# Attention stage of a decoder trunk: softmax weights added up before one sum by ones, half of the cache pages on TensorE's column strips, pages alone on SyncE's queue

## The chip, the cores and the metric

The kernel runs on 1 core of a Trainium2 chip. The metric is the device time of one execution in microseconds. Engines by their names in the profile: PE is TensorE (PEld its weight loads), DVE VectorE, ACT ScalarE, POOL GpSimd, SP SyncE.

## What is computed

One inference step of a two-layer decoder for a prompt of 2048 rows and for 8 sample sequences of one row each. Layer 0 has attention with forgetting (8 heads of 64) beside a gated MLP; layer 1 is an mLSTM. The change lies in the attention of layer 0, in which the prompt attends to itself and each sample row to 64 pages of 128 cached positions:

```python
def fox_block(q, k, v, cq, ck, qpos, kpos):
    s = jnp.einsum('bqhd,bkhd->bhqk', q, k).astype(F32) * (q.shape[-1] ** -0.5)
    s = s + cq.swapaxes(1, 2)[:, :, :, None] - ck.swapaxes(1, 2)[:, :, None, :]
    s = jnp.where(kpos[None, :] <= qpos[:, None], s, -jnp.inf)
    p = jax.nn.softmax(s, axis=-1)
    return jnp.einsum('bhqk,bkhd->bqhd', p.astype(v.dtype), v)
# prompt: blocks of queries against the prompt's own k, v
# sample: v_all = concatenate([cache_v[page_table], v]) : 8 sequences x 64 pages x 128 positions x 512
y = jnp.concatenate([ya, yb], -1) @ w_out      # ya = att * silu(za); then the residual is added
```

## The kernel before

`build` runs `even_project` (input projection of layer 0, and the scores of the sample rows against the cached keys), `decode_softmax` (softmax of these scores, left in `keep["scores"]`: for each page and head one weight per cached position, positions on the 128 partitions), `attend`, and `mlstm` (layer 1). Only `attend` is changed. It does three things in one block, on all engines at once:

- *Prompt attention.* Queries go in 4 groups of 512 rows, heads in 4 pairs: 16 units (`UN`). A unit of group g has 4(g+1) key slots (`count`), 160 slots in all (`STEPS`). In slot i TensorE computes the scores of 128 keys by up to 512 queries for both heads of the pair into `S2` (`score_keys`, two heads on the two row halves of the array), ScalarE turns them into weights `PT` (`exp`, L992), and a slot later TensorE multiplies by the values into `O` (L1215) and sums the weights over the keys by a matrix of ones into `Z` (L1217) (`product`). Before a unit's keys come, its queries' maxima are needed: `score_queries` computes scores the other way round into `S1` (one buffer), VectorE takes maxima (`maximum`, L1050), both for the next unit, spread over the slots of this one (`p1_end`). At a unit's end `gate` multiplies `O` by the gate, `invert` makes 1/Z on ScalarE by Ln and Exp, `normalise` multiplies.
- *Output projection* of the group before (`project`, L1235, `y_at`: 24 of them in slots, 8 in a tail of 8 steps), with the `residual` added on VectorE and read and written by GpSimd's DMAs.
- *Cached values of the sample rows.* 512 pages of [128 x 512] are loaded in pairs into a ring of five (`vpage`, `RING`), multiplied by the weights and added up in `acc` by VectorE (`page_pair`, L1100 and L1103). Of every fourth pair ScalarE does the products (`scale_page`, L1007, 16 activations a pair). At a sequence's end a turn `d` sums over the partitions by ones.

Every engine's order is written out by the Python loops at build time. "Turns" are uses of TensorE's and ScalarE's shared bank `T` (transposes of staged k, q and x rows, and small sums); turn e waits for the evacuation of turn e-1. Where pages stand is set by `spare` and `pair_end`: the pairs are shared out over the slots in proportion to an estimate of TensorE's time, so that a slot with a projection has 4 pairs, others mostly 1. SyncE's queue holds in one order the loads of stage rows (ring of 4), of the values `V` and of the pages, each behind the wait for its buffer. Slots of units 4, 5, 8, 9, 12 and 13 hold the projections.

## Time and profile before

| | us |
|---|---|
| median of 3 runs | 3806.46 (3800.5 to 3808.48) |
| the profiled execution | 3808.97 |
| its span | 3806.8 |
| PE busy in the span | 3324.9 (87%) |
| DVE busy | 2084.7 (55%) |
| ACT busy | 1047.5 (28%) |

The span is from the first to the last instruction of one execution; the execution's own time is 2.2 us longer. The stage of `attend` goes from about 1058 us (first memset of GpSimd) to about 2098 us, its 160 slots from 1090 to 2018 us. The page's busy tenths show all stages in 40 slices of 95 us; `attend` lies in slices 12 to 22, and the chain that ended last lies wholly in the last stage, since the stages are parted by barriers. "Idle before" of a group is the time for which the engine stood ahead of its instructions, with who released it.

### The profile page before, as it was taken

How to read it: one execution, taken by the hardware profiler on the slowest of the kernel's cores; microseconds unless marked ns; L12 is line 12 of the kernel's file. 1: busy time of each engine (PE TensorE's matmuls, PEld its weight loads, DVE VectorE, ACT ScalarE, POOL GpSimd, SP SyncE). 2: the span in 40 equal slices, each digit the busy share in tenths (PEclk: the TensorE clock that was granted, in tenths of full speed). 3: DMA queues.
4: the chain of work that ended last, by engine and by line, in shares of the span. 5: the costliest groups of instructions: out<-in, count | busy, mean ns of one | idle time of the engine just before them, and what ended most of it. 6: DMA issues, size and time to landing. Idle time of an engine off the chain costs nothing. (4 is left out here: it accounts for less than half of the span.)

```text
span 3806.8 us, 44892 instructions
## 1 busy us (share of the span) xinstructions
PE 3324.9 (87%) x14087; PEld 1795.8 (47%) x14087; DVE 2084.7 (55%) x3066; ACT 1047.5 (28%) x2520; POOL 120.7 (3%) x221
## 2 busy tenths in 40 slices
PE   2999999999269888999888499999999999667799
PEld 1444444444134333333333276767767767412343
DVE  1778887888447776887786043443444434313211
ACT  1111111110145554554463122223222322103111
POOL 0000000000010000000000000000000000000000
PEclk8999999999679999999999699999999999877899
DMA  5566666665155644645555500000000000425232
GB/s 212 173 194 195 193 201 197 195 203 178 67 158 182 195 134 152 184 143 178 160 164 169 195 12 11 22 11 11 22 11 11 22 11 12 22 77 155 95 110 73
DMA packets 243054, 448.06 MB, mean 118 GB/s; under 512 B 38529, under 2 KB 69249, under 8 KB 241850
## 3 DMA queue, kind: packets, MB, share of 16 engines
q1 hardware_dynamic: 222602, 412.12, 35.9%
q0 software_dynamic: 5696, 18.88, 1.4%
q10 hardware_dynamic: 14592, 15.24, 1.2%
q8 instruction: 58, 0.95, 0.1%
q14 instruction: 106, 0.87, 0.1%
HBM read 390.16 MB, written 55.99 MB: 117 GB/s over the span
## 5 line engine op out<-in xcount | busy, mean ns | idle before, releaser
L523 PE MATMUL ep_PJ<-ep_w,ep_xT 128*128 128x512 f32 x1792 | 781.9, 595 | 10.4 <-ACT ep_xT L383 10.4
L523 PEld LDWEIGHTS ep_PJ<-ep_w,ep_xT 128*128 128x128 f32 x1792 | 337.5, 190 | 420.3 <-issue 413.9
L1734 PE MATMUL mb_B<-ml_w,mp_xT 128*128 128x512 f32 x1024 | 446.4, 594 | 0.0
L444 DVE TENSOR_TENSOR ep_kpage<-ep_kpage,ep_q_bc 128x1024 f32<-128x1024 f32 x256 | 311.5, 1217 | 128.9 <-DMA ep_kpage<-in_cache_k_dram 128.6
L1007 ACT ACTIVATE at_vpage<-at_vpage,g_scores 128x64 f32<-128x64 f32 x1008 | 253.1, 338 | 262.3 <-DMA at_vpage<-in_cache_v_dram 262.3
L452 DVE TENSOR_REDUCE g_scores<-ep_kpage 128x1024 f32 (+1 forms) x256 | 311.6, 1217 | 11.5 <-DVE ep_kpage L444 3.3
L1103 DVE TENSOR_TENSOR at_acc<-at_acc,at_vpage 128x1024 f32<-128x1024 f32 x240 | 293.7, 1224 | 18.3 <-ACT at_vpage L1007 8.8
L1734 PEld LDWEIGHTS mb_B<-ml_w,mp_xT 128*128 128x128 f32 x1024 | 192.0, 190 | 230.1 <-issue 229.6
L1050 DVE TENSOR_REDUCE at_mpart<-at_S 128x2 f32<-128x1024 f32 (+3 forms) x160 | 170.3, 1065 | 220.2 <-PE at_S L1172 132.1
L1747 PE MATMUL mb_B<-mp_xT,ml_w 128*128 128x128 f32 x2048 | 252.3, 289 | 0.0
L1747 PEld LDWEIGHTS mb_B<-mp_xT,ml_w 128*128 128x128 f32 x2048 | 249.8, 205 | 0.0
L2252 PE MATMUL fi_O<-ml_w,fi_yT 128*128 128x512 f32 (+1 forms) x544 | 237.6, 595 | 0.0
L1100 DVE TENSOR_TENSOR at_vpage<-at_vpage,g_scores 128x1024 f32<-128x1024 f32 x185 | 225.3, 1218 | 0.0
L992 ACT ACTIVATE at_PT<-at_S,g_negc 128x512 f32<-128x512 f32 (+3 forms) x320 | 180.6, 615 | 161.6 <-PE at_S L1200 161.2
L1190 PE MATMUL at_S<-at_QT,at_KT 64*128 64x512 f32 (+3 forms) x640 | 165.9, 596 | 58.4 <-ACT at_PT L992 58.4
L1169 PE MATMUL at_S<-at_KT,at_QT 64*128 64x512 f32 (+3 forms) x640 | 159.9, 578 | 23.8 <-DVE at_mpart L1050 23.7
L1617 DVE SCALAR_TENSOR_TENSOR mp_cv<-mp_xcT,ml_cw,mp_cv 128x128 f32<-128x128 f32 x384 | 105.1, 347 | 132.5 <-ACT mp_cv L1532 131.3
L2252 PEld LDWEIGHTS fi_O<-ml_w,fi_yT 128*128 128x128 f32 (+1 forms) x544 | 99.4, 185 | 126.6 <-issue 126.5
L1215 PE MATMUL at_O<-at_PT,at_V 128*64 128x512 f32 (+3 forms) x640 | 152.2, 554 | 2.5 <-issue 2.5
L1217 PE MATMUL at_Z<-at_PT,g_ones 128*64 128x512 f32 (+3 forms) x640 | 144.0, 528 | 0.0
L1190 PEld LDWEIGHTS at_S<-at_QT,at_KT 64*128 64x128 f32 x640 | 50.7, 190 | 160.1 <-ACT at_PT L992 94.3
L2223 DVE TENSOR_TENSOR fi_o<-fi_h,fi_O 128x512 f32<-128x512 f32 (+1 forms) x34 | 21.8, 683 | 184.3 <-PE fi_O L2252 184.3
(447 smaller groups left out, 3613.6 us busy)
## 6 DMA issues: line engine op xcount, KB each, us to landing
ep_kpage<-in_cache_k_dram SPq DMA_DIRECT2D x512, 256.0 KB, 3.0
at_vpage<-in_cache_v_dram SPq DMA_DIRECT2D x512, 256.0 KB, 3.0
ep_w<-in_even_w_in_dram SPq DMA_DIRECT2D x8, 1796.0 KB, 30.7
ml_w<-in_odd_w_in_dram SPq DMA_DIRECT2D x24, 512.0 KB
ep_x<-in_x_prompt_dram SPq DMA_DIRECT2D x16, 512.0 KB
scratch_mix<-ep_mixed SPq DMA_DIRECT2D x16, 512.0 KB, 3.0
at_stage<-scratch_mix SPq DMA_DIRECT2D x32, 256.0 KB, 3.5
at_xh<-in_x_prompt_dram POOLq DMA_DIRECT2D x32, 256.0 KB, 3.5
```

The source lines that it names most:

```text
L444: nc.vector.tensor_tensor(kpage[i][:], kpage[i][:], q_bc[r][:].unsqueeze(1).to_broadcast([P, 2, AW]), ALU.mult).then_inc(pr[i], 1)
L452: op = nc.vector.tensor_reduce(dst, kpage[i][:].rearrange("p j (h d) -> p j h d", h=AH), AX.X, ALU.add)
L523: op = nc.tensor.matmul(BANK[name][:], xT[r][:, k, :], w[:, k, COL[name]:COL[name] + 512], start=k == 0, stop=k == KC - 1)
L992: nc.scalar.activation(PT[i % 3][:, hh, 0:n], S2[:, hh, 0:n], ACT.Exp, bias=keep["negc"][:, j, h:h + 1]).then_inc(exped, 1)
L1007: op = nc.scalar.activation(part, part, ACT.Copy, scale=keep["scores"][:, k // 32, h, p:p + 1])
L1050: nc.vector.tensor_reduce(mpart[:, qi, :, b], S1[:, :, 0:width], AX.X, ALU.max).then_inc(maxed, 1)
L1100: nc.vector.tensor_tensor(split(here), split(here), w, ALU.mult).then_inc(weighed, 1)
L1103: nc.vector.tensor_tensor(here if k % 32 == 31 else acc[:], acc[:], here, ALU.add).then_inc(added, 1)
L1190: nc.tensor.matmul(S2[:, hh, 0:n], KT[rows, hp, j * P:(j + 1) * P], QT[u % 3][rows, lo:512], start=True, stop=False, skip_group_check=True)
L1734: op = nc.tensor.matmul(B[banks[m]][:], xT[:, k, :], w[:, k, col + 512 * m:col + 512 * m + 512], start=k == 0, stop=k == KC - 1)
L1747: op = nc.tensor.matmul(B[c // 4][:, (c % 4) * P:(c % 4 + 1) * P], w[:, k, c * P:(c + 1) * P], xT[:, k, :], start=k == 0, stop=k == KC - 1)
L2252: op = nc.tensor.matmul(O[2 * r + m][0:n, :], yT[r][:, k, 0:n], w[:, k, 512 * m:512 * m + 512], start=k == 0, stop=k == KC - 1)
```

## The change

The ring of `PT` goes from 3 to 2, of stage rows from 4 to 3. `psum` (in SBUF) holds the sum of a unit's weights over its slots: VectorE copies the first and adds the others (`add_up`), and a new turn `z` at the start of the next unit sums `psum` by ones once into `T`; ScalarE takes Ln and Exp from there. `L1217` goes. Of the pages two of every four stay with VectorE (128 pairs, ring of 2 pairs), all their products now on VectorE; `scale_page` goes. The other two pages, in groups of four (64 groups, ring of 3 pairs in `spage`), are multiplied on TensorE: the weights [128 x 8 heads] are the stationary operand, the page moves, and each of the four pages of a group has its own 32 columns of the array and rows of the bank `D`. At a sequence's end `pick_heads` keeps each head's own 64 columns, and the turn `d` adds them in. SyncE's queue holds pages alone; the loads of stage rows and of `V` move to GpSimd's queue, behind its masks and among the residual's reads and writes. VectorE's order within a slot changes: `add_up` of the slot before, then pages, then `gate` and further maxima.

```diff
-        RING = 5
-        PT = [s.sb(f"PT{i}", [P, 2, 512]) for i in range(3)]
-        stage = [s.sb(f"stage{i}", [P, AW]) for i in range(4)]
+        PT = [s.sb(f"PT{i}", [P, 2, 512]) for i in range(2)]
+        psum = s.sb("psum", [P, 2, 512])
+        stage = [s.sb(f"stage{i}", [P, AW]) for i in range(3)]
-        vpage = [s.sb(f"vpage{i}", [P, 2, AW]) for i in range(RING)]
+        vpage = [s.sb(f"vpage{i}", [P, 2, AW]) for i in range(2)]
+        spage = [s.sb(f"spage{i}", [P, 2, AW]) for i in range(3)]
-            n = slot2(i)[3]
             p1 = p1_end[i] - (p1_end[i - 1] if i else first[1])
-            return (n * 2.1 + n * 3.4) / 1000 + 0.3 + 1.2 * p1 + 7.1 * len(y_at[i])
+            return slot2(i)[3] * 3.9 / 1000 + 0.3 + 1.2 * p1 + 7.1 * len(y_at[i])
+        PAIRS = NB * PAGES // 4
+        GROUPS = PAIRS // 2
+        SEQ_P, SEQ_G = PAIRS // NB, GROUPS // NB
+        whole = sum(pe_us(i) for i in range(STEPS + TAIL - 3))
+            while nd < min(PAIRS, round(PAIRS * so_far / whole)) and nd <= SEQ_P * (ready + 1):
+                nd += 1
+            while ns < min(GROUPS, int(GROUPS * so_far / whole)) and ns < SEQ_G * (ready + 1):
+                ns += 1
+            loads_at[i] += [("v", d + 2) for d in in_step(d_end, i) if d + 2 < PAIRS]
+            loads_at[i] += [("s", 2 * g + r) for g in in_step(s_end, i) for r in (3, 4) if 2 * g + r < 2 * GROUPS]
+            if i == STEPS or i and i < STEPS and i == first[unit_of[i]]:
+                late[i] = [len(turns)]
+                turns.append(("z", (unit_of[i] if i < STEPS else UN) - 1, 0))
...
         def _(sp):
+            def weighed_pair(d):
+                if d >= 2:
+                    sp.wait_ge(added, d - 1)
+                    if (d - 2) % SEQ_P == SEQ_P - 1:
+                        sp.wait_ge(turned, d_turn[(d - 2) // SEQ_P] + 1)
                 for j in range(2):
+                    page(4 * d + j, vpage[d % 2][:, j, :], vp_in[d % 2])
+            def strip_pair(n):
+                if n >= 3:
+                    sp.wait_ge(paged, 4 * ((n - 3) // 2 + 1))
+                for j in range(2):
+                    page(4 * n + 2 + j, spage[n % 3][:, j, :], sp_in[n % 3])
             for i in range(STEPS + TAIL):
+                for kind, n in loads_at[i]:
+                    if kind == "v":
+                        weighed_pair(n)
+                    else:
+                        strip_pair(n)
...
         def _(pool):
+            nc.gpsimd.memset(own_head[:], 0.0).then_inc(const, 1)
+            for strip in range(4):
+                rows = slice(32 * strip, 32 * strip + 32)
+                nc.gpsimd.affine_select(out=own_head[rows, :], in_=own_head[rows, :], compare_op=ALU.not_equal, fill=1.0,
+                                        base=0, pattern=[[-1, AH]], channel_multiplier=1).then_inc(const, 1)
+            for i in range(STEPS + TAIL):
+                while got < len(loads) and loads[got] < t_end[min(i + 2, STEPS + TAIL)]:
+                    stage_in(got)
+                    got += 1
+                if i % 8 == 0 and 1 <= i // 8 < GR:
+                    values_in(i // 8)
+                for y in y_at[i]:
+                    residual_out(y)
+                    if y + 2 < 2 * NT:
+                        residual_in(y + 2)
...
         def _(act):
+                elif kind == "z":
+                    if a:
+                        act.wait_ge(gated, a)
+                    nc.scalar.activation(rc[:], T[:], ACT.Ln).then_inc(evac, 1)
+                    act.wait_ge(evac, e + 1)
+                    nc.scalar.activation(rc[:], rc[:], ACT.Exp, scale=-1.0).then_inc(inverted, 1)
             def exp(i):
-                if i >= 3:
-                    act.wait_ge(used, 2 * (i - 2))
+                if i >= 2:
+                    act.wait_ge(used, 2 * (i - 1))
+                    act.wait_ge(summed, i - 1)
             for i in range(STEPS):
-                if i > 1 and i - 1 == first[unit_of[i - 1]]:
-                    invert(unit_of[i - 1] - 1)
                 exp(i)
+                for e in held:
+                    evacuate(e)
+                held = late[i] if turns[t_end[i + 1] - 1][0] == "z" else []
-                for k, j in scale_at[i]:
-                    scale_page(k, j)
...
         def _(dve):
+            def add_up(i):
+                u, j, lo, n = slot2(i)
+                dve.wait_ge(exped, 2 * (i + 1))
+                if j == 0:
+                    if u:
+                        dve.wait_ge(turned, z_turn[u - 1] + 1)
+                    nc.vector.tensor_copy(psum[:], PT[i % 2][:]).then_inc(summed, 1)
+                else:
+                    dve.wait_ge(summed, i)
+                    nc.vector.tensor_tensor(psum[:, :, lo:512], psum[:, :, lo:512], PT[i % 2][:, :, 0:n], ALU.add).then_inc(summed, 1)
+            def pick_heads(b):
+                dve.wait_ge(paged, 4 * SEQ_G * (b + 1))
+                nc.vector.tensor_tensor(strip_sum[:].rearrange("p (h d) -> p h d", h=AH), D[:].rearrange("p (h d) -> p h d", h=AH),
+                                        own_head[:].unsqueeze(2).to_broadcast([P, AH, AD]), ALU.mult).then_inc(masked, 1)
+                for n in todo[:1]:
+                    maximum(n)
+                if 1 <= i <= STEPS:
+                    add_up(i - 1)
+                if 1 < i < STEPS and i - 1 == first[unit_of[i - 1]]:
+                    normalise(unit_of[i - 1] - 1)
+                for d in in_step(d_end, i):
+                    page_pair(d)
+                for b in range(NB):
+                    if closed[b] == i:
+                        pick_heads(b)
+                if i == STEPS or i and i < STEPS and i == first[unit_of[i]]:
+                    gate((unit_of[i] if i < STEPS else UN) - 1)
+                if i == STEPS:
                     normalise(UN - 1)
+                for n in todo[1:]:
+                    maximum(n)
...
         def _(pe):
+                elif kind == "z":
+                    pe.wait_ge(summed, first[a + 1])
+                    for hh, rows in enumerate(halves):
+                        op = nc.tensor.matmul(T[rows, :], keep["ones"][:, 0:AD], psum[:, hh, :], start=True, stop=True, skip_group_check=True)
-                for hh, rows in enumerate(halves):
-                    nc.tensor.matmul(Z[rows, lo:512], keep["ones"][:, 0:AD], PT[i % 3][:, hh, 0:n], start=j == 0, stop=last,
                                      skip_group_check=True).then_inc(used, 1)
+            def strips(g):
+                b = g // SEQ_G
+                if g % SEQ_G == 0:
+                    pe.wait_ge(masked, b + 1)
+                for r in range(2):
+                    n = 2 * g + r
+                    pe.wait_ge(sp_in[n % 3], 32 * (n // 3 + 1))
+                for strip in range(4):
+                    n, j = 2 * g + strip // 2, strip % 2
+                    p = (4 * n + 2 + j) % PAGES
+                    op = nc.tensor.matmul(D[32 * strip:32 * strip + AH, :], keep["scores"][:, b, :, p], spage[n % 3][:, j, :],
+                                          start=g % SEQ_G == 0, stop=g % SEQ_G == SEQ_G - 1, skip_group_check=True)
+                    op.then_inc(paged, 1)
                 for y in y_at[i]:
                     project(y)
+                for g in in_step(s_end, i):
+                    strips(g)
                 if i:
                     product(i - 1)
```

## Rows read from the trace of the kernel before

**Rows 1.** Busy time of the engines in stretches, clock, DMA share, GB/s.
```profile
core 0: us, PE busy (x) PEld busy (x) DVE busy (x) ACT busy (x) POOL busy (x), PEclk, DMA share, GB/s
1380.00:1574.00 194.00, 166.55 (x734) 67.56 (x736) 132.71 (x132) 86.19 (x260) 8.72 (x16) 0.93 0.53 160
sum 1040.00, PE 915.51 PEld 382.06 DVE 745.46 ACT 527.04 POOL 44.49; mean PE 83.23 PEld 34.73 DVE 67.77 ACT 47.91 POOL 4.04
```
**Rows 2.** Groups by line, 1055 to 2095 us: busy us, mean ns | idle before.
```profile
L1103 DVE TENSOR_TENSOR at_acc<-at_acc,at_vpage 128x1024 f32<-128x1024 f32 x240 | 293.7, 1224 | 18.3 <-ACT at_vpage L1007 8.8
L1007 ACT ACTIVATE at_vpage<-at_vpage,g_scores 128x64 f32<-128x64 f32 x1008 | 253.1, 338 | 262.3 <-DMA at_vpage<-in_cache_v_dram 262.3
L1100 DVE TENSOR_TENSOR at_vpage<-at_vpage,g_scores 128x1024 f32<-128x1024 f32 x185 | 225.3, 1218 | 0.0
L1050 DVE TENSOR_REDUCE at_mpart<-at_S 128x2 f32<-128x1024 f32 (+3 forms) x160 | 170.3, 1065 | 220.2 <-PE at_S L1172 132.1 <-PE at_S L1179 87.3
L1217 PE MATMUL at_Z<-at_PT,g_ones 128*64 128x512 f32 (+3 forms) x640 | 144.0, 528 | 0.0
```
**Rows 3.** TensorE's waits, 1090 to 2020 us: us in total, times, longest.
```profile
PE at_S L1190 <- ACT at_PT L992: 58.4, 28, 6.6
PE at_S L1169 <- DVE at_mpart L1050: 21.3, 33, 2.6
```
**Rows 4.** Timeline of a late page in slot 50: start, us, instruction.
```profile
1397.33 2.02 ACT L1007 ACTIVATE at_vpage<-at_vpage,g_scores 128x64 f32<-128x64 f32 x8 [5.60 <-DMA at_vpage<-in_cache_v_dram]
1400.55 2.08 PE L1190 MATMUL at_S<-at_QT,at_KT 64*128 64x512 f32 x4 [5.79 <-ACT at_PT L992]
```
**Rows 5.** Timeline of a warm plain slot, 1588 to 1593 us.
```profile
1588.13 1.13 PE L1190 MATMUL at_S<-at_QT,at_KT 64*128 64x512 f32 x4
1589.54 1.27 ACT L992 ACTIVATE at_PT<-at_S,g_negc 128x512 f32<-128x512 f32 x2 [2.57 <-PE at_S L1200]
1590.48 1.08 PE L1215 MATMUL at_O<-at_PT,at_V 128*64 128x512 f32 x4
1591.39 1.03 PE L1217 MATMUL at_Z<-at_PT,g_ones 128*64 128x512 f32 x4
1592.35 1.13 PE L1190 MATMUL at_S<-at_QT,at_KT 64*128 64x512 f32 x4
```
**Rows 6.** Timeline of the sample rows' projection on four column strips.
```profile
59.68 1.07 PE L288 MATMUL ep_PJ<-ep_w,ep_xT 128*8 128x512 f32 x8
60.55 0.59 PE L288 MATMUL ep_TR<-ep_w,ep_xT 128*8 128x512 f32 x1
```
**Rows 7.** Timeline: a table load in an inversion, and the first tail projection.
```profile
1580.20 1.28 ACT L1000 ACT_TABLE_LOAD   x1
2030.81 5.27 PE L1235 MATMUL at_Y<-g_w_out,at_yA 128*128 128x512 f32 x8 [10.64 <-DVE at_yA L1084]
```
**Rows 8.** Timeline of the stage's start.
```profile
1058.63 2.65 SPq L889 DMA_DIRECT2D at_stage<-out_k_prompt_dram  x4
1062.00 1.11 PE L1156 MATMUL at_T<-g_ident,at_stage 128*128 128x128 f32 x4 [20.67 <-DMA at_stage<-out_k_prompt_dram]
1066.06 2.15 POOL L943 TENSOR_SCALAR_AFFINE_SELECT at_sel<-at_sel 64x128 bf16<-64x128 bf16 x8
1068.16 1.18 POOL L949 DMA_DIRECT2D at_xh<-in_x_prompt_dram  x2
```
**Rows 9.** Timeline from a projection's last matmuls to the next residual's read.
```profile
1409.05 3.60 PE L1235 MATMUL at_Y<-g_w_out,at_yB 128*128 128x512 f32 x8
...
1414.94 0.68 DVE L1108 TENSOR_TENSOR at_xh<-at_xh,at_Y 128x512 f32<-128x512 f32 x1
...
1415.91 0.54 POOL L955 DMA_DIRECT2D scratch_h<-at_xh  x1 [110.26 <-DVE at_xh L1108]
...
1419.50 0.55 POOL L949 DMA_DIRECT2D at_xh<-in_x_prompt_dram  x1 [3.04 <-DMA scratch_h<-at_xh]
```
**Rows 10.** SyncE issuing eight pages; a stage load's size and time to landing.
```profile
1199.20 8.05 SPq L901 DMA_DIRECT2D at_vpage<-in_cache_v_dram  x8
...
at_stage<-out_k_prompt_dram SPq DMA_DIRECT2D x16, 256.0 KB, 3.6
```

More of the change, by code:

```diff
@@ L903, in _ @@
[L903 to L916 removed]
+            sp.wait_ge(pages_in, 16)
@@ L1002, in scale_page @@
[L1002 to L1008 removed]
+                    nc.scalar.activation(PT[i % 2][:, hh, 0:n], S2[:, hh, 0:n], ACT.Exp, bias=keep["negc"][:, j, h:h + 1]).then_inc(exped, 1)
@@ L1247, in _ @@
                     score_queries(n)
-                here = list(range(t_end[i], t_end[i + 1]))
-                for e in here:
-                    if turns[e][0] != "m":
+                for e in range(t_end[i], t_end[i + 1]):
+                    if e not in late[i]:
                         turn(e)
@@ L1257, in _ @@
                     score_queries(n)
-                for e in here:
-                    if turns[e][0] == "m":
-                        turn(e)
+                for e in late[i]:
+                    turn(e)
             product(STEPS - 1)
```

226 lines of the change are left out of this document (95 added, 131 removed).

## Prediction

> **What bounds the kernel now.** I read the span first (3806.8 us, one core), then the busy tenths of the page: only the stage of `attend`, from 1058 to 2098 us, has the lines of the change. Over these 1040 us TensorE is busy 915.5, VectorE 745.5, ScalarE 527.0 us, at a granted clock of 0.93 in the stretch from 1380 to 1574 [rows 1]. So TensorE sets the pace, but not alone: some 125 us of the stage it stands, and part of the time it runs at 1.2 GHz. Next the groups, for the prices of one instruction [rows 2]. Then the waits inside the 160 key slots (1090 to 2020): TensorE waited 58.4 us for ScalarE's exponentials and 21.3 us for VectorE's maxima [rows 3]. The exponentials are not slow; what stands ahead of them on ScalarE is. In the timeline `scale_page` gets its page 5.60 us late, the exponential behind it is late, TensorE's `score_keys` starts after 5.79 us of idling, and its four matmuls then take 2.08 us [rows 4] where a warm slot's take 1.13 [rows 5]: each such wait also costs clock. Going through the 28 waits in the timeline, all but about 2 us follow a scaled page.
>
> A warm plain slot of full width takes 4.22 us from `score_keys` to `score_keys`: 1588.13 to 1592.35, of it `L1217`, the sum by ones, from its middle at 1591.39 to the next slot, 0.96 us with the change of weights [rows 5]. Slots with an output projection take 7.0 us more.
>
> **The change, part by part.**
>
> *Sum by ones off TensorE's slots.* Widths of all 160 slots add up to 136 full ones; 136 x 0.96 = 131 us, 128 with the shorter gaps of the narrow slots: -128 us. Back comes one sum for a unit, 16 x 0.96 = +15 us.
>
> *Strips.* 64 groups of four matmuls, [128 x 8] weights, 512 float32 columns, in column strips 0, 32, 64, 96. The trace has such a group: in the sample rows' projection four matmuls (eight instructions) start at 59.68 and the next strip group at 60.55: 0.87 us for four, not for one [rows 6]. With 0.1 us for the change of tile form (a slot's sum by ones takes 0.96, 0.09 over 0.87) a group costs 0.97: 60 of them lie in the slots, +58 us. Closing a sequence takes 12 instead of 8 one-column matmuls, each with a full weight load: about 0.9 us more, 8 times, +7 us. TensorE's work in the slots: -128 + 15 + 58 + 7 = -48 us. Bounds of a group: 0.87 and, if strips ran one after another, 4 x 0.87 = 3.5 (a rival below). The Trainium skill, "TensorE: Matmul & The Clock Gate" (section "The cost: per-tile semaphore tail"), puts some 26 ns on every semaphore increment of a tile and each strip has one; by its figure an estimate of 64 x 3 x 0.026 = 5 us would be added. No row here separates that.
>
> *ScalarE.* 1008 activations, 253.1 us, and the 262.3 us of waiting for pages before them, go [rows 2]. The 56 us that TensorE stood for late exponentials go with them. Of the lost clock: 0.93 over 194 us means 14% of the time at 1.2 GHz, some 13 us lost; the same reading over all stretches of the slots gives 28 us. Other idling will keep some of it; I take -18, bounds -28 and 0. What is late next is VectorE.
>
> *VectorE.* Page work was 248 + 8 + 185 operations of 1.22 us, 539 us; now 128 pairs with 248 operations, 303 us. New are 160 additions of the weights (two SBUF inputs, as in `L1103`, 1.224 us for 1024 elements [rows 2]): 136 x 1.22 + a little for narrow ones = 172 us, and 8 products by heads, 5 us. In sum -59 us. But they are distributed otherwise. The planner now gives a pair to 74 plain slots and none to 59, where before nearly each had one, half at one operation. A plain slot with a pair holds 1.22 (maximum) + 1.22 (addition) + 2.5 = 4.9 us of VectorE against 3.3 of TensorE (4.22 - 0.96), without a pair 2.45 against 3.3, and two of five have a strip group (+1.0). Means: VectorE 3.9, TensorE 3.7. There is one slot of slack at most: `S1` has one buffer (`score_queries` waits for the maximum before), `PT` now two, and the exponential waits for the addition two slots back. Playing slots 128 to 136 through with these durations gives about 4.1 us a plain slot. 0.4 us over TensorE's work, in some 115 slots without projection, is 46 us; 21 us of waits for maxima exist already [rows 3]: +25. At the first slot of a unit the order is worse: `gate` and the second maximum now stand behind the pair (before, ahead of it). The second maximum ends about 8.5 us after the slot's start, TensorE wants the next `S1` at about 7.2: 1.3 us, in slots 24 and 60 with two pairs some 4; with the new turn `z`, whose bank ScalarE frees only after the next exponential and a table load (1.28 us [rows 7]), this is +12 in 15 units. VectorE term +37; bounds +10 (it overlaps with TensorE's strips) and +75. In slots with a projection TensorE has 11.3 us and VectorE 8.3: it is hidden there. The last unit has no maxima; there the loop `score_keys` to end of exponentials (1588.13 to 1589.54 + 1.27 = 2.68 us [rows 5]) binds before TensorE's 2.2 us; 0.5 x 16 = 8 us is in the 46.
>
> *Copy against GpSimd.* Sixteen additions are float32 copies in SBUF. The trace has no such copy; by the nearest row of 1024 elements 1.22, at least half that. The Trainium skill, "SBUF — State Buffer" (section "SBUF: two separate sides"), says that GpSimd can't write the descriptors of its DMAs while VectorE runs such a copy. It speaks against having both in this change. By it a load waits at most for one copy, and 16 x 1.22 = 20 us would be the most it could cost. No run here shows it yet.
>
> *Loads of stage, values on GpSimd's queue.* 64 loads and 4 of values leave SyncE. First, the start: SyncE issued the first `k` load at 1058.63 and TensorE turned it at 1062.00. GpSimd is busy with masks until 1068.16, where its first DMA was issued [rows 8]. A fifth memset and four more selects at 0.27 us each, with a wait, add 1.5: first load at 1069.7, first turn 3.4 us later, 1073.1 against 1062.0. Nothing else runs then: +11 us (bounds +8, +14). Only three stage buffers: the fourth load waits for the first turn and lands 0.5 + 3.5 us later, just in time. Second, in the slots: behind a projection GpSimd waits for `residual`, writes, waits for the landing, reads the next residual, and only then issues the next stage load. In the trace: projection ends at 1412.65, `residual` starts 1414.94, write 1415.91, read 1419.50 [rows 9], then 0.55 + 3.6 us to landing [rows 10]: 11.5 us after the projection. A turn two slots later comes after about 8.5 us. So 3 us for each turn that stands two slots behind a projection; slots 22, 29, 55, 63, 71, 108, 111 and perhaps two that are near, mostly shortened by other waits: 6 x 2.5 = +15 us. Bounds 0 and +40.
>
> *Pages on SyncE.* 512 pages at 1.1 us (eight in 8.05 us [rows 10]) are 564 us: not the bound. But the queue is in order: a strip pair is issued behind a weighed pair that waits for VectorE. With strip groups two slots apart (88 and 90, nearly 32 and 34, 72 and 74, 128 and 130) the pair is issued 9.8 us after the slot's start, with 2.2 + 3 us to land at 15, and TensorE wants it at 11. All in all +8 us, bounds 0 and +25. A late page now blocks TensorE itself.
>
> *Tail.* Before the last projections TensorE stood 10.64 us [rows 7], since ScalarE had three scaled pages ahead of the inversion. After: the turn `z` 0.96, two table loads and two activations 3.8, `normalise` 0.7, with a strip group inside: about 6.5. -4 us.
>
> **Sum.** -48 (work) - 56 (late exponentials) - 18 (clock) + 37 (VectorE) + 15 (stage loads) + 8 (page order) + 11 (start) - 4 (tail) = -55 us. The profiled execution took 3808.97 us (span 3806.8 and 2.2 around it), so 3754; it lies 2.5 us above the median of 3806.46. Forecast 3752.
>
> **The rivals.**
> 1. *The waits overlap.* VectorE's, GpSimd's and the page waits fall together and the clock stays up: VectorE +15, others +8. -48 - 56 - 25 + 15 + 8 + 11 - 4 = about -95: 3712. For it: in the slots with projections, where most of the 58 us arose, VectorE is now clearly shorter. Against: a plain slot has little slack.
> 2. *VectorE takes over.* The pair of 4.9 us sits in the slot's middle, `S1` turns round once a slot: VectorE +70, stage loads +20, which gives -17: 3790. For it: all of VectorE's new 172 us lie on the way from an exponential to the next but one. Against: its total falls by 59 us.
> 3. *Slower: GpSimd's one queue.* If every one of the 22 turns in units with projections waits, and the clock falls each time as in [rows 4] (idle 5.8 us, then 2.7 us of slow clock), a turn costs up to 5 us: +110 instead of +15, i.e. +40: 3846. It decides from 3.2 us per turn ((55 + 15) / 22) on. Against: most turns are loaded one slot ahead of the projection's chain, and a neighbouring projection covers 7 us.
> 4. *The strips don't run side by side.* Their weights are columns 65 elements apart and each strip has its own moving page. Then +2.6 us x 64 = 166, less what VectorE's slots hide, say 140: 3892. Against: rows 6, where four matmuls ran at once with different moving data.
>
> **How the numbers follow.** Forecast 0.50, rival 1 0.19, rival 2 0.17, rival 3 0.10, rival 4 0.04. The range takes in rivals 1 and 2 and the terms' bounds, 3708 to 3803; 3 and 4 are out, 0.14, and a bit of the edges. 0.2% (7.6 us, about what a measurement of this kernel can tell from no change): slower 0.11 (3 has a part in the middle), the same 0.06 (mostly the end of rival 2), faster 0.83.
>
> **What would show it.** Right: no activations on pages, waits of `L1190` for ScalarE below 15 us; a strip group about 1 us; the sum by ones 16 times; TensorE's waits for VectorE's maxima up from 21 to about 50 us; the first turn about 11 us later; waits of turns for stage loads of some 15 us; VectorE busy about 685 us in the stage; the stage about 985 us long. Wrong: strip groups of 3 us, a granted clock in the slots that is not higher than before, waits of TensorE for pages above 25 us, or stage loads landing later than 4 us after issue on GpSimd's queue.

## The result, and the profile after

The changed kernel is slower: 3892.36 us, median of 4 runs (3891.27 to 3896.33), against 3805.84 us of the kernel before on the same chip, ratio 1.0231 with a 95% interval of 1.0213 to 1.0249. The profiled execution has a span of 3894.6 us; before it was 3806.8. Of these 88 us, 11 are the stage's start and 85 the 160 key slots; 5 come back between the last slot and the first projection of the tail, 3 in the rest. (Later kernels were timed in groups, each beside the kernel before, whose median was 3804 to 3809 us in them. So differences of medians between groups are good to some 5 us; the ratios are the safer.)

The stage's slots as a whole, first of before (1090 to 2018 us), then of after (1101 to 2114 us). Columns as in [rows 1].

```profile
1090.00:2018.00 928.00, 837.63 (x4442) 344.56 (x4440) 694.76 (x710) 497.53 (x1391) 26.18 (x48) 0.97 0.55 167
```

```profile
1101.00:2114.00 1013.00, 844.49 (x4399) 327.70 (x4398) 642.08 (x700) 279.56 (x458) 60.96 (x106) 0.91 0.50 155
```

This pair says most of it. TensorE got less work and is busy 7 us longer, at a granted clock of 0.91 instead of 0.97. And from the first to the last `score_keys` it stands 168.5 us instead of 90.4. VectorE and ScalarE are both busy for less time than before, as was meant. So no engine ran out of capacity; something makes TensorE stand.

Its waits after, between 1090 and 2120 us (us in total, times, longest), which answer to [rows 3]:

```profile
PE at_D L1280 <- DMA at_spage<-in_cache_v_dram: 67.3, 19, 9.9
PE at_S L1222 <- DVE at_mpart L1076: 35.4, 27, 4.3
PE at_T L1209 <- DMA at_stage<-scratch_q_prompt: 16.9, 3, 6.8
PE at_T L1200 <- ACT at_yB L1026: 12.9, 5, 3.9
PE at_T L1209 <- ACT at_rc L1009: 8.7, 5, 2.5
PE at_T L1209 <- DMA at_stage<-scratch_mix: 7.6, 2, 4.7
PE at_T L1209 <- DMA at_stage<-out_k_prompt_dram: 6.5, 1, 6.5
PE at_S L1243 <- ACT at_PT L1036: 5.7, 13, 2.1
```

The 58.4 us of late exponentials are down to 5.7. In their place stand 67.3 us for pages of the strips, a wait that the kernel before can't have: there a late page stopped VectorE or ScalarE, now it stops TensorE. Stage rows that come late cost 31.0 us (16.9 + 7.6 + 6.5) instead of 5.2. A fourth wait is new and easily passed over: turns that wait until ScalarE has emptied bank `T`, 28.7 us in all (12.9, 8.7 and 7.1 in smaller rows) where it was 1.4 before. 8.7 of it stand behind the inversion of turn z; where the rest comes from is shown at c2 and e8.

The groups of after by line, 1055 to 2185 us, for those of [rows 2] (busy us, mean ns | idle before, releaser). The first two rows are of before (1055 to 2098 us), for `score_keys` and for the product with the values; their counterparts of after, with the same work, are the two rows behind them:

```profile
L1190 PE MATMUL at_S<-at_QT,at_KT 64*128 64x512 f32 (+3 forms) x640 | 165.9, 596 | 58.4 <-ACT at_PT L992 58.4
L1215 PE MATMUL at_O<-at_PT,at_V 128*64 128x512 f32 (+3 forms) x640 | 152.2, 554 | 2.5 <-issue 2.5
L1243 PE MATMUL at_S<-at_QT,at_KT 64*128 64x512 f32 (+3 forms) x640 | 175.3, 627 | 5.8 <-ACT at_PT L1036 5.7
L1267 PE MATMUL at_O<-at_PT,at_V 128*64 128x512 f32 (+3 forms) x640 | 163.2, 591 | 0.0
L1121 DVE TENSOR_TENSOR at_psum<-at_psum,at_PT 128x1024 f32<-128x1024 f32 (+3 forms) x144 | 149.7, 1040 | 6.6 <-ACT at_PT L1036 6.0
L1134 DVE TENSOR_TENSOR at_vpage<-at_vpage,g_scores 128x1024 f32<-128x1024 f32 x120 | 146.3, 1219 | 39.2 <-DMA at_vpage<-in_cache_v_dram 39.1
L1280 PE MATMUL at_D<-at_spage,g_scores 128*8 128x512 f32 x512 | 75.1, 660 | 69.7 <-DMA at_spage<-in_cache_v_dram 69.7
L1191 PE MATMUL at_T<-g_ones,at_vpage 128*128 128x1 f32 x128 | 20.6, 265 | 1.6 <-ACT at_KT L1026 1.0 <-DVE at_strip_sum L1145 0.7
L1196 PE MATMUL at_T<-at_psum,g_ones 128*64 128x512 f32 x64 | 20.5, 723 | 1.6 <-DVE at_psum L1121 1.6
L1192 PE MATMUL at_T<-g_ones,at_strip_sum 128*128 128x1 f32 x64 | 12.8, 269 | 0.0
L1118 DVE COPY at_psum<-at_PT 128x1024 f32<-128x1024 f32 x16 | 10.9, 684 | 1.0 <-PE at_T L1196 1.0
```

The strips do what they should. In the timeline (start, us, instruction) the product behind a group starts 0.99 us after it:

```profile
1705.78 1.05 PE L1280 MATMUL at_D<-at_spage,g_scores 128*8 128x512 f32 x8
...
1706.77 1.08 PE L1267 MATMUL at_O<-at_PT,at_V 128*64 128x512 f32 x4
```

Where the time goes is best seen in slot 60, the one behind the slot that closes a sequence; 5.6 us before, 21.2 now:

```profile
1535.11 0.36 PE L1192 MATMUL at_T<-g_ones,at_strip_sum 128*128 128x1 f32 x2
1535.51 0.17 ACT L1005 ACTIVATE g_s_dec<-at_T 128x4 f32<-128x4 f32 x1 [2.55 <-PE at_T L1192]
1536.31 4.00 SPq L892 DMA_DIRECT2D at_vpage<-in_cache_v_dram  x4
1540.62 1.22 DVE L1134 TENSOR_TENSOR at_vpage<-at_vpage,g_scores 128x1024 f32<-128x1024 f32 x1 [6.30 <-DMA at_vpage<-in_cache_v_dram]
1541.10 3.63 SPq L892 DMA_DIRECT2D at_spage<-in_cache_v_dram  x4
...
1545.36 1.90 PE L1280 MATMUL at_D<-at_spage,g_scores 128*8 128x512 f32 x8 [9.88 <-DMA at_spage<-in_cache_v_dram]
...
1547.81 2.08 PE L1222 MATMUL at_S<-at_KT,at_QT 64*128 64x512 f32 x4
```

Read it from the top. TensorE sums the closed sequence (turn d). Only then does SyncE ask for the weighed pairs, because `weighed_pair` waits for that turn before it may write over the buffer with the closing sum. The four strip pages stand behind them in SyncE's queue, asked for at 1541.10, and TensorE, which wanted them at 1535.5, gets them at 1545.36. It has stood 9.88 us and then runs its group in 1.90 us instead of 1.05 and the next scores in 2.08 instead of 1.13.

SyncE's own waits between 1090 and 2120 us show what its queue is held by. The first row is VectorE's pairs, the second turn d, the third the strip groups that still read the buffer:

```profile
SPq L891 <- DVE at_acc L1137: 312.5, 95, 14.1
SPq L898 <- PE at_T L1192: 124.7, 7, 30.9
SPq L891 <- PE at_D L1280: 29.4, 12, 4.5
```

### The profile page after: what moved, and what is told of

Same layout as the page of the kernel before. It is cut to its first block and busy times, and to the rows that moved or that the text cites. A ratio compares the mean times of both kernels' runs of the same rounds, so it can differ in the third digit from the quotient of the medians.

```text
span 3894.6 us, 43985 instructions
## 1 busy us (share of the span) xinstructions
PE 3334.3 (86%) x14087; PEld 1778.0 (46%) x14087; DVE 2012.4 (52%) x3042; ACT 810.8 (21%) x1512; POOL 162.2 (4%) x294
## 5 line engine op out<-in xcount | busy, mean ns | idle before, releaser
L1222 PE MATMUL at_S<-at_KT,at_QT 64*128 64x512 f32 (+3 forms) x640 | 161.6, 584 | 35.6 <-DVE at_mpart L1076 35.4
L1243 PE MATMUL at_S<-at_QT,at_KT 64*128 64x512 f32 (+3 forms) x640 | 175.3, 627 | 5.8 <-ACT at_PT L1036 5.7
L1134 DVE TENSOR_TENSOR at_vpage<-at_vpage,g_scores 128x1024 f32<-128x1024 f32 x120 | 146.3, 1219 | 39.2 <-DMA at_vpage<-in_cache_v_dram 39.1
L1267 PE MATMUL at_O<-at_PT,at_V 128*64 128x512 f32 (+3 forms) x640 | 163.2, 591 | 0.0
L1121 DVE TENSOR_TENSOR at_psum<-at_psum,at_PT 128x1024 f32<-128x1024 f32 (+3 forms) x144 | 149.7, 1040 | 6.6 <-ACT at_PT L1036 6.0
L1137 DVE TENSOR_TENSOR at_acc<-at_acc,at_vpage 128x1024 f32<-128x1024 f32 x112 | 137.2, 1225 | 3.8
L1280 PE MATMUL at_D<-at_spage,g_scores 128*8 128x512 f32 x512 | 75.1, 660 | 69.7 <-DMA at_spage<-in_cache_v_dram 69.7
L1209 PE MATMUL at_T<-g_ident,at_stage 128*128 128x128 f32 x256 | 47.3, 314 | 80.5 <-DMA at_stage<-out_k_prompt_dram 39.4
```

The lines of the kernel that those rows point to most:

```text
L1121: nc.vector.tensor_tensor(psum[:, :, lo:512], psum[:, :, lo:512], PT[i % 2][:, :, 0:n], ALU.add).then_inc(summed, 1)
L1222: nc.tensor.matmul(S1[:, hh, 0:width], QT[u % 3][rows, qi * P:(qi + 1) * P], KT[rows, hp, 512 * b:512 * b + width], start=True, stop=False ...
L1243: nc.tensor.matmul(S2[:, hh, 0:n], KT[rows, hp, j * P:(j + 1) * P], QT[u % 3][rows, lo:512], start=True, stop=False, skip_group_check=True)
L1267: nc.tensor.matmul(O[rows, lo:512], V[:, j, h * AD:(h + 1) * AD], PT[i % 2][:, hh, 0:n], start=j == 0, stop=last, skip_group_check=True).t ...
```

## The experiments

The theory after the result: the loss is a loop. Late pages and late stage rows make TensorE stand, each stand lowers its clock, and VectorE, which does maxima, additions and page pairs in one queue, passes its own lateness on through the maxima. The rivals: one part alone is to blame, the pages' order on SyncE's queue (called theory P in the expectations), the loads on GpSimd's queue (G), the additions on VectorE (V) or the shorter ring of `PT`. The table gives what the runs measured; "slots" is from the first to the last `score_keys`, the clock is that of 1100 to 2000 us, and the last three columns are TensorE's waits between 1090 and 2120 us for maxima, strip pages and stage rows.

| kernel | us | ratio to before | slots us | clock | maxima | strips | stage |
|---|---|---|---|---|---|---|---|
| before | | | 927.4 | 0.97 | 21.3 | | 5.2 |
| after | 3892.4 | 1.0231 (1.0213 to 1.0249) | 1012.6 | 0.91 | 35.4 | 67.3 | 31.0 |
| e1 strips first | 3881.3 | 1.0184 (1.0158 to 1.0209) | 999.7 | 0.92 | 64.8 | 18.8 | 31.3 |
| e2 stage on ScalarE | 3860.2 | 1.0144 (1.0120 to 1.0168) | 982.6 | 0.92 | 28.3 | 79.3 | |
| e3 no strip loads | 3819.5 | 1.0036 (1.0026 to 1.0047) | 933.6 | 0.94 | 50.3 | | 15.1 |
| e4 sum alone | 3909.7 | 1.0269 (1.0238 to 1.0299) | 1027.8 | 0.90 | 51.1 | | 13.9 |
| e5 no additions | 3841.5 | 1.0097 (1.0069 to 1.0124) | 951.7 | 0.93 | 19.1 | 68.3 | 28.2 |
| e6 two buffers | 3806.4 | 1.0008 (0.9997 to 1.0020) | 925.7 | 0.97 | 21.0 | | 5.2 |
| e7 closing sum in acc | 3862.8 | 1.0143 (1.0126 to 1.0160) | 968.0 | 0.93 | 47.8 | 30.0 | 26.1 |
| c1 = e1 + e2 | 3840.5 | 1.0099 (1.0080 to 1.0118) | 968.6 | 0.93 | 60.8 | 19.7 | |
| c4 = e1 + e2 + e7 | 3849.6 | 1.0104 (1.0087 to 1.0121) | 977.2 | 0.93 | 79.0 | 8.8 | |
| c3 all pages on strips | 3779.6 | 0.9924 (0.9907 to 0.9941) | 895.1 | 0.97 | 9.1 | | 9.1 |
| c2 = c3 + e2 | 3760.4 | 0.9880 (0.9863 to 0.9897) | 888.5 | 0.98 | 6.7 | | |
| e8 = c2, no additions | 3746.7 | 0.9838 (0.9822 to 0.9855) | 867.4 | 0.99 | 6.6 | | |

**e1: strip pages asked for first.** The changed kernel with one line moved.

```diff
-            loads_at[i] += [("v", d + 2) for d in in_step(d_end, i) if d + 2 < PAIRS]
             loads_at[i] += [("s", 2 * g + r) for g in in_step(s_end, i) for r in (3, 4) if 2 * g + r < 2 * GROUPS]
+            loads_at[i] += [("v", d + 2) for d in in_step(d_end, i) if d + 2 < PAIRS]
```

> The changed kernel with one edit: in each slot SyncE issues the loads of strip pairs ahead of those of weighed pairs, so a strip pair no longer stands behind the wait for VectorE's additions, nor behind the wait for the turn d of the sequence just closed. Theory P (page order on SyncE's queue): TensorE's 69.7 us of waits at the strips fall below 20 us, the granted clock in the slots rises from 0.90 to above 0.94, and the time falls from 3892 to about 3810 (3790 to 3830). Theory G (stage loads on GpSimd's queue set the loss): the time falls by less than 20 us. Theory V (the additions of the weights on VectorE set it): less than 20 us as well.

Measured: 3881.3, 11 us less, far from the 3810 that theory P expected, though the waits for strip pages fell below 20 us as it said: by 48.5 us, while those for maxima rose by 29.4. The lateness was handed on: VectorE now waits 80.4 us for its pages (39.1 in after), and the maxima stand behind those. The two waits for pages in this kernel, 1050 to 2160 us:

```profile
DVE at_vpage L1134 <- DMA at_vpage<-in_cache_v_dram: 80.4, 18, 8.1
PE at_D L1280 <- DMA at_spage<-in_cache_v_dram: 18.8, 7, 7.3
```

**e2: stage rows and values on ScalarE's queue.** The changed kernel; each load is issued where the turn that frees its buffer is evacuated.

```diff
             def evacuate(e):
                 kind, a, half = turns[e]
                 act.wait_ge(turned, e + 1)
+                if e in load_no and load_no[e] + 3 < len(loads):
+                    stage_in(load_no[e] + 3)
```

> The changed kernel with the loads of stage rows and values moved from GpSimd's to ScalarE's queue: a load is issued as soon as the turn that frees its buffer is done. Strips and pages are as changed. Theory G: the first turn is 11 us earlier, the 31 us of waits of turns for stage loads in the slots go, and with the clock that they cost the time falls by 60 us or more, to 3832 or below. Theory P: 11 us at the start and some 20 to 30 us in the slots, 3850 to 3865; the strips' waits stay near 70 us. Theory V: 11 us and little more.

Measured: 3860.2, 32 us less. The waits for stage rows are gone, the first slot starts 12.8 us earlier, at 1088.4, and the slots take 30.0 us less. That is theory P's range for it (3850 to 3865), not G's. The waits for strip pages rose by 12, which fits that TensorE now comes to them sooner; and those for ScalarE to empty bank `T` rose from 28.7 to 36.0, which fits that ScalarE now issues the loads in between.

**e3: no loads for the strips.** The changed kernel that loads three strip pairs and never again, so that 250 of the strip pages are left out; all matmuls remain.

```diff
-            loads_at[i] += [("s", 2 * g + r) for g in in_step(s_end, i) for r in (3, 4) if 2 * g + r < 2 * GROUPS]
...
-                    pe.wait_ge(sp_in[n % 3], 32 * (n // 3 + 1))
+                    pe.wait_ge(sp_in[n % 3], 32)
```

> The changed kernel without the loads of strip pages after the first three pairs: 250 page loads and their waits on SyncE's queue are left out, the strips multiply the same six pages again and again. It shows what the lateness of strip pages costs in all. Theory P: the waits at the strips go entirely, and the time falls by 90 us or more, to about 3795. Theory G and V: by less than 25 us.

Measured: 3819.5, 73 us less and within 0.4% of before. It is the largest step of e1 to e7, and lies between the theories (P: 90 or more, G and V: under 25). It comes near the 67.3 us of waits, but the maxima are waited for longer (50.3 us instead of 35.4). And it also takes half of SyncE's issues and of the traffic away (DMA share 0.34 instead of 0.50), so it bounds the cost of late strip pages from above; it doesn't say why they are late.

**e4: the sum alone.** The kernel before, with only the weights added on VectorE and summed once, and the ring of `PT` at two; pages, their scaling on ScalarE and all loads are as before.

```diff
-                    nc.tensor.matmul(Z[rows, lo:512], keep["ones"][:, 0:AD], PT[i % 3][:, hh, 0:n], start=j == 0, stop=last,
-                                     skip_group_check=True).then_inc(used, 1)
...
+                    for n in todo[:1]:
+                        maximum(n)
+                    if i:
+                        add_up(i - 1)
```

> The kernel before with one part of the change alone: the weights of a unit are added up on VectorE and summed once by ones (two buffers of weights instead of three); pages, rings, queues and ScalarE's page products stay as before. TensorE's work falls by 113 us, VectorE's grows by 172 us on top of 745 in a stage of 1040. Theory V: VectorE becomes the bound and the time is above 3806, 3830 or more. Theories P and G: the additions are not what makes the changed kernel slow; the time is within 30 us of 3806, on either side, as VectorE's load of 917 us nearly fills the stage.

Measured: 3909.7, slower than before by 104 us, and at least as slow as the whole change. This though the slots' sums by ones have left TensorE (144.0 us busy in [rows 2], about 20 back for turn z). Stretch 1100 to 2000 us of this kernel (columns as in [rows 1]) and three of its waits between 1050 and 2160 us:

```profile
1100.00:2000.00 900.00, 711.53 (x3372) 292.73 (x3374) 722.75 (x755) 428.22 (x1203) 26.27 (x48) 0.90 0.50 151
```

```profile
PE at_S L1219 <- ACT at_PT L1007: 113.7, 47, 11.3
ACT at_PT L1007 <- DVE at_psum L1106: 83.9, 31, 5.1
PE at_S L1198 <- DVE at_mpart L1061: 53.5, 47, 5.2
```

VectorE is busy 80% of the time, no more; yet the exponentials wait for its additions, TensorE waits for exponentials twice as long as before (58.4), and for maxima more than twice as long (21.3).

**e5: no additions.** The changed kernel without its 144 additions; the first tile of each unit is still copied (plus 1e-6), so the row sums cover that tile alone.

```diff
-                else:
-                    dve.wait_ge(summed, i)
-                    nc.vector.tensor_tensor(psum[:, :, lo:512], psum[:, :, lo:512], PT[i % 2][:, :, 0:n], ALU.add).then_inc(summed, 1)
...
-                    act.wait_ge(summed, i - 1)
+                    act.wait_ge(summed, unit_of[i - 2] + 1)
```

> The changed kernel with 144 of the 160 additions of weights left out: VectorE copies each unit's first slot (plus 1e-6) and adds nothing; the sum by ones and the inversion stay, and an exponential no longer waits for an addition two slots back. All queues as changed. Theory V (the additions on VectorE, in the order of its queue, lengthen the slots): TensorE's waits for maxima fall from 35 us to below 15, ScalarE's for the additions vanish, and the time falls from 3892 by 60 us or more, to 3830 or below. Theory P (page order on SyncE and the stage loads explain the loss): these waits stay and the time falls by less than 25 us.

Measured: 3841.5, 51 us less (theory V wanted 60 or more, P less than 25), with TensorE's waits for maxima down to 19.1 and those for ScalarE to empty bank `T` down from 28.7 to 11.8. Still 0.97% slower than before: even at no cost for the sum, the pages and loads of this change lose.

**e6: two buffers of `PT`.** The kernel before with its ring of three cut to two, as the change has it.

```diff
-        PT = [s.sb(f"PT{i}", [P, 2, 512]) for i in range(3)]
+        PT = [s.sb(f"PT{i}", [P, 2, 512]) for i in range(2)]
```

> The kernel before with two buffers of weights instead of three, nothing else. It tells the price of the shorter ring, which the changed kernel and e4 both have, from that of the additions. If the ring is what made e4 slow, the time is 3850 or more; if the additions are, it is within 8 us of 3806. Theory V expects the latter: with the sum by ones in the slot, the buffer of two slots back is free long before the exponential wants it.

Measured: ratio 1.0008, an interval that holds 1. By itself the shorter ring costs nothing. That doesn't clear it where the additions are: there a buffer is free only when its addition is done, and ScalarE's exponentials waited 116.3 us for additions in the changed kernel (1050 to 2160 us) and 83.9 in e4. A third buffer beside the additions wasn't run, so what the ring adds to their price stays open.

**e7: the closing sum stays in `acc`.** The changed kernel; SyncE no longer waits for turn d, VectorE does before the next sequence's first product, and the planner gives that product to a slot behind the close at the earliest.

```diff
-            while nd < min(PAIRS, round(PAIRS * so_far / whole)) and nd <= SEQ_P * (ready + 1):
+            while nd < min(PAIRS, round(PAIRS * so_far / whole)) and nd < SEQ_P * (ready + 1):
...
-                    if (d - 2) % SEQ_P == SEQ_P - 1:
-                        sp.wait_ge(turned, d_turn[(d - 2) // SEQ_P] + 1)
...
+                        dve.wait_ge(turned, d_turn[b - 1] + 1)
...
-                    nc.vector.tensor_tensor(here if d % SEQ_P == SEQ_P - 1 else acc[:], acc[:], here, ALU.add).then_inc(added, 1)
+                    nc.vector.tensor_tensor(acc[:], acc[:], here, ALU.add).then_inc(added, 1)
```

> The changed kernel in which the closing sum of a sequence's weighed pages stays in the accumulator instead of going into a buffer of the page ring, so that SyncE no longer waits for turn d of the closed sequence before it loads the pair after it; VectorE waits for that turn instead before the next sequence's first product, which may come at the earliest one slot later. Theory (the order and the waits on SyncE's queue cost about 70 us, and the seven to eight waits for turn d, 124.7 us in SyncE's queue, are their largest part): 3840 to 3865 us, TensorE's waits for strip pages down from 69.7 us to under 40, and the slots after a close back from 14 to 20 us to about 6. Rival (the strip pages are late because VectorE is late with its pairs, whatever stands between): 3880 to 3895, and the waits for strip pages stay above 55 us.

Measured: 3862.8, 30 us less (slots 45 less), within the theory's 3840 to 3865. The 124.7 us of SyncE's waits are gone, those for strip pages fell to 30.0, and the slots behind a close came back: slot 24 from 20.6 to 8.0 us, 60 from 21.2 to 8.8, 101 from 18.6 to 8.0, 118 from 15.9 to 7.6. So this one wait, in seven places, carries a third of the loss when it alone goes. (The 30 us are net of VectorE's new wait for turn d and of the first product's later slot.)

**c1 and c4: the repairs together.** c1 is e1 and e2; c4 is e1, e2 and e7.

> Both edits at once on the changed kernel: stage rows and values on ScalarE's queue (32 us faster alone), strip pairs ahead of weighed pairs on SyncE's (11 us faster alone). If the two add up: about 3849. If the strip pages were late partly because other waits hid behind them, more: Theory P expects 3830. Theory V expects no less than 3840, since what is left is VectorE's.

> The changed kernel with three repairs of its loads and no other change: strip pages are asked for ahead of VectorE's, the staging rows come through ScalarE's queue, and the closing sum stays in the accumulator, so that SyncE waits for no turn. The first two together gave 3840.5. Theory (with the page waits gone, what is left over the kernel before is VectorE's additions and pages in one queue, 50 us by the run without additions): 3815 to 3835, slower than before by 10 to 30 us, with TensorE's waits for partial maxima at 50 us or more. Rival (late pages are still what matters, and VectorE would keep up with them): 3780 to 3805, with those waits under 30 us.

Measured: 3840.5 and 3849.6. c1 lies at the end of the range of theory V (no less than 3840); c4 missed its 3815 to 3835. The third repair brought nothing on top of the two (ratios 1.0099 and 1.0104). The late strip pages are nearly gone in c4, but the maxima are later than in any other kernel (waits between 1050 and 2160 us):

```profile
PE at_S L1217 <- DVE at_mpart L1070: 81.4, 38, 8.0
DVE at_vpage L1129 <- DMA at_vpage<-in_cache_v_dram: 64.7, 19, 6.6
PE at_D L1275 <- DMA at_spage<-in_cache_v_dram: 8.8, 4, 2.7
```

What is left, 1.0%, is for the most part in VectorE's queue: it waits for its own pages, asked for last, with maxima and additions behind them. Another 37.5 us are turns that wait for ScalarE to empty bank `T`.

**c3, c2 and e8: VectorE without pages.** c3 is the changed kernel with all 512 pages on the strips, in 128 groups of four pages, and a ring of three such groups; `page_pair`, `vpage` and `acc` are gone. c2 also has the stage loads on ScalarE's queue. e8 is c2 without the additions, with row sums of each unit's first tile alone.

```diff
+            def group(g):
+                if g >= 3:
+                    sp.wait_ge(paged, 4 * (g - 2))
+                for j in range(4):
+                    page(4 * g + j, spage[g % 3][:, j, :], sp_in[g % 3])
...
-                for d in in_step(d_end, i):
-                    page_pair(d)
```

> All 512 pages on TensorE's column strips (128 groups, ring of three groups), none on VectorE; weights of a unit still added up on VectorE; stage rows and values on ScalarE's queue. TensorE's work grows by another 62 us over the changed kernel, VectorE's falls by 303. Theory V: with VectorE at about 380 us in the stage nothing waits for it, the slots take TensorE's sum of some 815 us plus 40 for page and bank waits, against 927 before, and the kernel is faster than before: 3740 (3715 to 3770). Theory P: page supply on SyncE (4.4 us a group, in one order) now stands ahead of TensorE everywhere: waits at the strips above 60 us and a time of 3800 or more.

> The changed kernel with all 512 pages on the four strips (128 groups, a ring of three groups of four pages), no page on VectorE, and the loads of the staging rows left on GpSimd's queue as in the changed kernel. The same with those loads on ScalarE's queue took 3760.4. Theory (VectorE's load, the pages' order and the stage loads are three parts whose costs overlap while waits are shared): the stage loads cost here 15 to 30 us, since each late load now meets a TensorE with no other wait to hide behind: 3775 to 3792. Rival (the loop through VectorE was all of it, and the stage loads only mattered as part of it): 3760 to 3772.

> The kernel with all pages on strips and the staging rows on ScalarE's queue (3760.4), without the 144 additions of weights on VectorE; only the first key tile of each unit is copied. The row sums are left out of the computation but for that tile. Theory (an addition of 1.2 us costs nothing where VectorE is busy 372 of 900 us and TensorE sets the pace): 3750 to 3762. Rival (the additions lie on the way from exponentials to maxima whatever VectorE's load): 3700 to 3725, as in the changed kernel, where they cost 51 us.

Measured: c2 3760.4, 1.2% faster than before and the best of the kernels with the whole computation; c3 3779.6; e8 3746.7. c2 from 1100 to 2000 us:

```profile
1100.00:2000.00 900.00, 850.17 (x4778) 314.78 (x4775) 371.70 (x466) 280.96 (x458) 27.28 (x50) 0.98 0.58 177
```

And its strips between 1055 and 2098 us, 128 groups of four, without any idle time before them:

```profile
L1231 PE MATMUL at_D<-at_spage,g_scores 128*8 128x512 f32 x1024 | 133.5, 611 | 0.0
```

Four readings. TensorE has 64 strip groups more than in the changed kernel and is 132 us faster; VectorE, at 372 of 900 us, is hardly ever late (6.7 us of waits for maxima), and no wait for a page shows. The ring is deeper too (three groups of four pages instead of one and a half), but c4 shows that strip pages asked for first are nearly in time with the short one (8.8 us). The loads on GpSimd's queue cost 19 us here (c3 against c2), of which 12 are the start, 1103.3 instead of 1091.1. The additions cost 13.7 us (e8; 16 by the ratios, 21 in the slots of the profiled executions), slightly more than expected (up to 10), where they cost 51 in the changed kernel: their price is set by what else is in VectorE's queue. And what is left of the price has its place in the traces: from c2 to e8 TensorE stands 13.5 us less in the slots (47.3 to 33.8), and its waits for ScalarE to empty bank `T` fall by just that, from 34.2 to 20.7, while those for maxima (6.7 and 6.6) and exponentials (5.0 and 5.0) stay. One such turn, three rows of c2 and then the same turn in e8:

```profile
1395.67 0.37 ACT L1005 ACTIVATE at_PT<-at_S,g_negc 128x128 f32<-128x128 f32 x1 [4.79 <-DVE at_psum L1096]
...
1396.18 0.60 ACT L995 ACTIVATE at_yB<-at_T 128x512 f32<-128x512 f32 x1
...
1396.84 0.40 PE L1154 MATMUL at_T<-g_ident_bf,at_pc 128*128 128x128 bf16 x4 [2.21 <-ACT at_yB L995]
```

```profile
1388.63 0.40 PE L1151 MATMUL at_T<-g_ident_bf,at_pc 128*128 128x128 bf16 x4 [0.49 <-ACT at_yB L995]
```

The exponential waits for an addition, ScalarE empties `T` only behind it, and TensorE's next turn waits 2.21 us instead of 0.49. The 11.3 us behind the inversions of turn z are in both kernels.

## Why the prediction was wrong, point by point

The forecast was 55 us faster; it came out 86 slower. By its own steps:

- *Start, +11*: right. The first turn started at 1072.97 (1073.1 was worked out), the first `score_keys` 11.05 us later than before.
- *Tail, -4*: right. From the last `score_keys` to the first projection 13.3 us became 8.1.
- *Late exponentials, -56*: right in themselves, 58.4 to 5.7.
- *Strip group, 0.97*: right where TensorE is warm, 0.99; rival 4 is out, though its 3892 is the time measured. Averaged over slow and warm ones it is 75.1 / 64 = 1.17. Turn d was mis-sized: its two groups are busy 20.6 + 12.8 = 33.4 us against 15.5 before, +18 instead of +7.
- *Clock, -18*: wrong in sign. (1 - 0.97) x 928 = 28 us of full speed were lost before and (1 - 0.91) x 1013 = 91 are now, +63 at most, since part of it may fall into idle time. The work of -48 turned into +7 of busy time, 55 us apart; of these about 11 + 5 are turns d and z above their estimates. Slower matmuls are most of the rest: `score_keys`, `score_queries` and the product, whose work didn't change, are busy 175.3, 161.6 and 163.2 us instead of 165.9, 159.9 and 152.2, 22 us more, and the strips 75.1 instead of 64 x 0.97 = 62, 13 more. The step that failed is that lost clock was counted as belonging to the waits removed, and the waits added were allowed at most to keep it (bound 0), not to add to it, though [rows 4] had shown wait and lost clock together.
- *Page order, +8, bounds 0 and 25*: this is the step that failed most. It was put at 8 and measured 67.3 us of waits; without the strip loads the kernel is 73 us faster (e3). The prediction looked for strip groups close to each other behind VectorE. It passed over a wait that stands in the diff, two lines in `weighed_pair`: the pair two behind a sequence's closing pair waits for turn d, which TensorE runs one slot later, and every strip page is asked for behind it. e7 shows that wait to be worth 30 us. The other strip waits are those that the step meant, only more of them (13 are left in e7).
- *Stage loads, +15, bounds 0 and 40*: right in kind and low. The waits went from 5.2 to 31.0 us; with the start the two terms were 26, and e2 measured 32, c3 against c2 19.
- *VectorE, +37, bounds 10 and 75*: the waits for maxima rose by 14 us only, but e5 gives 51 us for the additions and e4 104 and more for the sum with all pages as before. The bounds held it in the change itself. What failed is that it was sized slot by slot with every page in time. A late page stops VectorE for up to 8.6 us, and then the maximum of the next slot is late too, since all stand in one queue with one buffer of `S1` to give. The +12 in it for unit starts named the bank of turn z, and 8.7 us of waits stand behind its inversions. But TensorE's waits for ScalarE to empty `T` rose from 1.4 to 28.7 us, and 17 of these go with the additions (11.8 left in e5): the prediction has no term for turns that ScalarE empties late because its exponential waits for an addition.
- *Copy against GpSimd*: put at 20 us at most and left out of the sum; 0.29 us in the trace, as said below.

Rival 1's sum comes to -99, not to the "about -95" that it states; it decides nothing here. Rival 2 named the engine, rival 3 the side and a price per turn (up to 5 us) that the longest waits for stage rows did reach (6.8), but in six places, not 22. None named the strip pages. The list of signs did: waits for pages above 25 us and a clock not higher than before were both written down as what would show it wrong. The terms don't add up in the runs either: alone, e3, e5 and e2 take off 73, 51 and 32 us, together 156 where 86 were lost. They share the same stands, and a repair of one (e1, c4) moves part of the wait to the next. That is what the theory of a loop says. e1 and c4 show the lateness moving to the maxima. c2 shows that nothing is late once VectorE has no pages, but it changes several things at once (pages off VectorE, one order, a deeper ring), so it doesn't tell them apart. What a third buffer of `PT` would give wasn't tried; nor whether strips with pages of both kinds, but without the sum, would win.

## What to carry to other kernels

When an operand changes its engine, ask who now stands when it is late: before, a late page held up VectorE or ScalarE, now it stops TensorE and its clock. For every load, list from the code all that its queue waits for ahead of it, semaphore by semaphore, and not only the neighbours of its own kind. And price an addition to an in-order queue by what else can be late in that queue: the same 144 additions cost 14 to 21 us with VectorE 41% busy and no page in its queue, and 51 us with it 62% busy and pages in it. Follow such an addition through every engine that waits for it: here it held ScalarE's exponential, the exponential held the emptying of bank `T`, and that held TensorE.

## What the runs showed of the hardware that was not expected

A float32 copy in SBUF of 128 x 1024 took VectorE 0.68 us, where an addition of the same size took 1.22; the prediction had taken 1.22 for it, and half of that at least. (The Trainium skill, "VectorE: DVE Perf Modes", section "The perf-mode tier table (the rule you actually need)", gives a float32 `tensor_copy` in SBUF a rate of 2x and a `tensor_tensor` 1x; the trace, with 1.8 between them, about agrees.)

Of the 16 copies only one met a DMA that GpSimd was issuing, the load of a `q` tile; the other row is the next such load:

```profile
1108.43 1.04 POOL L960 DMA_DIRECT2D at_stage<-scratch_q_prompt  x1 [2.88 <-PE at_T L1209]
1108.49 0.68 DVE L1118 COPY at_psum<-at_PT 128x1024 f32<-128x1024 f32 x1
...
1116.73 0.75 POOL L960 DMA_DIRECT2D at_stage<-scratch_q_prompt  x1 [2.31 <-PE at_T L1209]
```

That issue took 1.04 us; the 15 others of this kind took 0.75 to 0.77, and in e1, e3, e5, e7 and c3 the same one stands out with 1.04. So the rule in the Trainium skill, "SBUF — State Buffer" (section "SBUF: two separate sides"), by which GpSimd can't write descriptors during such a copy, agrees with the trace where the two meet, at a price of 0.29 us; 15 copies met no issue, so most of the bound of 20 us was never at stake.

The clock lost more than the prediction took it to lose: with TensorE idle 17% of the slots (168.5 of 1013 us) instead of 10% (90.4 of 928) the granted clock went from 0.97 to 0.91, and in c2, with TensorE busy 850 of 900 us, it was 0.98. The idle share alone doesn't give the clock: e3 stood 11% of its slots (101.5 of 933.6 us) at 0.94, c3 6% (52.1 of 895.1) at 0.97, no more than before.
